# Window attention with v held in PE: probabilities divided before they are weighed, the norm's scale applied at the residual

## The reference, cut to what matters

```python
s = einsum('bnqgrd,bnkgd->bngrqk', q, k) * (HEAD_DIM ** -0.5)
s = where(mask, s, NEG_INF)
m = maximum(max(s, axis=-1, keepdims=True), sink)
p = exp(s - m)
w = p / (sum(p, axis=-1, keepdims=True) + exp(sink - m))
attn = einsum('bngrqk,bnkgd->bnqgrd', w, v)
...
mix = concatenate([rmsnorm(attn, norm_attn_out), rmsnorm(ssm, norm_ssm_out)], axis=-1)
x = x + mix @ w_out
```

## Time and profile before

| | |
|---|---|
| median of 3 runs | 3607.56 us (3603.56 to 3611.9) |
| the profiled execution | 3614.2 us, span of its trace 3612.4 us |
| mean granted clock of TensorE in it | 0.797 |
| weighing of step 0 to weighing of step 7 | 73.97 to 380.10 us |
| end of the last mixing of `mix_tokens` | 400.18 us |

### The profile page before, as it was taken

One profiled execution on the slowest core, in us unless ns is written; L12 is line 12 of the kernel. 1 busy time (PEld: TensorE's weight loads), 2 busy tenths in 40 slices (PEclk: granted clock), 3 DMA queues, 4 the chain that ended last, 5 costly groups with the idle time before them and its releaser, 6 DMA issues.

```text
span 3612.4 us, 35899 instructions
## 1 busy us (share of the span) xinstructions
PE 2437.9 (67%) x9537; PEld 1030.4 (29%) x9537; DVE 2217.7 (61%) x4968; ACT 1007.9 (28%) x3376; POOL 1335.4 (37%) x1236
## 2 busy tenths in 40 slices
PE   7999656268566755765676667566856775686676
PEld 4565344114112311321141114111411331142121
DVE  5322251756865785578567756875686579558754
ACT  1111021133233223322332333233223222332232
POOL 1000030034434444444444444444444444444532
PEclk8888677679778868986896689677967886897699
DMA  4111124099999999999999999999999999999998
GB/s 155 44 44 38 39 50 192 31 414 416 407 382 417 415 376 393 415 420 369 403 415 409 382 396 421 394 368 411 417 398 373 414 413 383 412 421 417 390 421 349
DMA packets 192622, 1212.41 MB, mean 336 GB/s; under 512 B 28952, under 2 KB 35416, under 8 KB 51688
## 3 DMA queue, kind: packets, MB, share of 16 engines
q0 software_dynamic: 156672, 1140.92, 77.9%
q1 hardware_dynamic: 35416, 69.28, 5.5%
q10 hardware_dynamic: 320, 0.07, 0.0%
HBM read 1194.51 MB, written 15.55 MB: 335 GB/s over the span
## 4 chain that ended last, share of the span: by engine, by line
DMA 30%; PE 22%; DVE 15%; issue 11%; ACT 4%; POOL 2%; SPq 0%; DVEq 0%; POOLq 0%; ACTq 0%; PEldq 0%
DMA uv_ring<-in_uv_table,idx 29%; PE ACC L1787 13%; PE TQ L1742 7%; DVE uv_ring L1630 5%; DVE S L1594 2%; DVE picks L1595 2%; DVE S L1593 2%; POOL uv_ring L1369 2%; PE OP L1723 1%; ACT dg L1463 1%; ACT dot L1456 1%; DMA wq<-in_w_query 1%; ACT dot L1446 1%; PE ACC L1777 0%; DVE pos L1525 0%
## 5 line engine op out<-in xcount | busy, mean ns | idle before, releaser
L1787 PE MATMUL ACC<-uv_ring,dg 128*64 128x512 f32 x4352 | 1485.8, 795 | 935.0 <-ACT dg L1463 934.0
L1369 POOL DMA_INDIRECT uv_ring<-in_uv_table,idx x1088 | 1264.9, 1163 | 1822.2 <-PE ACC L1787 1319.2
L1630 DVE CUSTOM_DVE_ANT_0 uv_ring<-uv_ring,xn 128x1024 f32<-128x1024 f32 x1088 | 1325.2, 1226 | 826.8 <-DMA uv_ring<-in_uv_table,idx 764.3
L1787 PEld LDWEIGHTS ACC<-uv_ring,dg 128*64 128x64 f32 x4352 | 345.0, 168 | 1955.9 <-ACT dg L1463 1422.0
L1446 ACT ACTIVATE dot<-dot 128x2 f32<-128x2 f32 x544 | 110.6, 203 | 1767.6 <-DVE dot L1630 1767.2
L1463 ACT ACTIVATE dg<-stack,dot 128x64 f32<-128x64 f32 x1088 | 328.5, 341 | 53.3
L1742 PEld LDWEIGHTS TQ<-glu_and_queries,wq 128*128 128x128 f32 x2304 | 267.8, 195 | 66.2 <-issue 66.2
L1742 PE MATMUL TQ<-glu_and_queries,wq 128*128 128x128 f32 x2304 | 281.9, 281 | 1.4 <-issue 1.2
L1456 ACT ACTIVATE dot<-gate,dot 128x1 f32<-128x1 f32 x1088 | 261.2, 287 | 17.7
L503 PE MATMUL PJ<-w_in,xT 128*128 128x512 f32 (+1 forms) x432 | 160.5, 532 | 1.6 <-DMA w_in<-in_w_in 1.6
L503 PEld LDWEIGHTS PJ<-w_in,xT 128*128 128x128 f32 x432 | 83.5, 194 | 80.6 <-issue 75.4
(11 more groups left out here) (318 smaller groups left out, 1760.3 us busy)
## 6 DMA issues: line engine op xcount, KB each, us to landing
uv_ring<-in_uv_table,idx POOLq DMA_INDIRECT x1088, 11.0
glu_and_queries<-in_w_glu SPq DMA_DIRECT2D x9, 1024.0 KB, 17.0
wq<-in_w_query SPq DMA_DIRECT2D x1, 8192.0 KB, 31.6
xt<-in_x SPq DMA_DIRECT2D x9, 512.0 KB, 3.5
xr<-scratch_x SPq DMA_DIRECT2D x9, 512.0 KB
w_in<-in_w_in SPq DMA_DIRECT2D x2, 2048.0 KB, 10.7
xk<-in_x SPq DMA_DIRECT2D x8, 512.0 KB, 3.3
scratch_x<-xk SPq DMA_DIRECT2D x8, 512.0 KB, 2.6
```

Source lines behind the costliest of these rows:

```text
L1369: pool.indirect_dma_start(out=ring[:, s_ % RING, :], out_offset=None, in_=a["uv_table"], in_offset=bass.IndirectOffsetOnAxis(ap=idx[:, s_: ...
L1630: V.tensor_tensor_reduce(row, row, xn[:, g, :], 1.0, 0.0, ALU.mult, ALU.add, dot[:, s_:s_ + 1]).then_inc(dots, 1)
L1787: ins = nc.tensor.matmul(ACC[GT * g:GT * (g + 1), b, :], dg[:, n % DG, :], ring[:, n % RING, D + 512 * b:D + 512 * b + 512], start=False, ...
```

## The change

Five things change together. (1) The weighing of v: PE holds v (a window's 128 keys by 64 of one group) and the turned probabilities stream, 512 columns at a time (four heads by 128 queries). There are 4 products in place of 16, and their result in `X` is already turned: 64 partitions for each group, (r, query) along the free side. So `turn_out` and its copy go. (2) The probabilities are divided before PE turns them: `normalise_probs` scales the 8 heads' 128x256 rows on DVE by `rden`, and PE's turning waits for `normed` where it waited for `probs_done`. (3) The norm's scale is applied where the residual is added (`scalar_tensor_tensor` with `rsa`). Its mean square comes from ACT's squares of `X` (`square_attention`) and four products of PE with a column of ones (`sum_squares`), between the scores and the mixing. (4) The scores are taken in the order group 0, group 1, group 0, and so on. (5) `g_attn` and the rows of `w_top` are laid out for the order (r, g), and `mix_samples` places its heads likewise, with as many transfers of the same sizes.

```diff
-        at2 = c.sb("at2", [P, AW])
-        aT = c.sb("aT", [P, AW // P, P])
+        sq = c.sb("sq", [P, REP, P])
+        aT = c.sb("aT", [P, REP, P])
+        ones = c.sb("ones", [P, 1])
         small = c.sb("small_a", [P, 8, HEADS])
         stat = c.sb("stat_a", [P, 8])
...
         weights, late = c.sem("weights_in"), c.sem("late_in")
...
                 load_tables(0, 0)
                 sp.dma_start(sink[:], a["sink"].to_broadcast([P, HEADS])).then_inc(late, 16)
...
                     rstd(t, ssx, msx, rsx, D, k["ssx_done"], k["msx_done"], k["rsx_done"])
 
                 def rstd_a(t):
-                    rstd(t, ssa, msa, rsa, AW, k["ssa_done"], k["msa_done"], k["rsa_done"])
...
 
                 def rotate(t, p):
 
@@ -306,15 +309,15 @@
                     k["roped"].mark(pool.tensor_tensor(x2, rt[:, 2], rt[:, 3], ALU.add))
 
                 def step(t, p, first=False, last=False):
+                    k["weighed"].held(pool, t - 1)
+                    k["v_kept"].mark(pool.tensor_copy(vb[:, p, :], pj[:, p, AW + KV * HD:U_COL]))
...
-                for n in ("ssx_done", "qkT_done", "probs_done", "ptr_act"):
+                for n in ("ssx_done", "qkT_done", "probs_done", "ptr_act", "sq_done"):
                     k[n].prime(act)
+
...
                     nc.scalar.activation(qT[:].rearrange("p r n -> p (r n)"), QK[:, 0:512], ACT.Copy)
                     k["qkT_done"].mark(nc.scalar.activation(kT[:, p, :], QK[:, 512:512 + P], ACT.Copy))
+                    if not first:
+                        square_attention(t - 1)
...
-                def divide(t):
+                def take_attention(t):
 
                     k["weighed"].of(dve, t)
-                    k["rden_done"].of(dve, t)
-                    k["at2_done"].of(dve, t - 1)
-                    k["at_done"].mark(nc.vector.tensor_tensor(
-                        at[:].rearrange("p (h d) -> p h d", d=HD), X[:].rearrange("p (h d) -> p h d", d=HD),
-                        bcast(rden, HD, 2), ALU.mult))
-                    k["at_done"].of(dve, t)
-                    k["a_turned"].of(dve, t - 1)
-                    k["ssa_done"].mark(nc.vector.tensor_tensor_reduce(at2[:], at[:], at[:], 1.0, 0.0,
-                                                                      ALU.mult, ALU.add, ssa))
-
-                def normalise_out(t):
-                    k["ssa_done"].of(dve, t)
-                    k["rsa_done"].of(dve, t)
-                    k["at2_done"].mark(nc.vector.tensor_scalar(at2[:], at[:], rsa, None, ALU.mult))
-
-                def take_out_columns(t):
-                    k["a_turned"].of(dve, t)
                     k["mixed"].of(dve, t - 1)
                     k["aT_done"].mark(nc.vector.tensor_tensor(
-                        aT[:], X[:].rearrange("p (k n) -> p k n", n=P), bcast(g_attn[:], P, 2), ALU.mult))
+                        aT[:], X[:].rearrange("p (r n) -> p r n", n=P), bcast(g_attn[:], P, 2), ALU.mult))
+
+                def mean_square(t):
+                    k["summed"].of(dve, t)
+                    k["rsa_done"].of(dve, t - 1)
+                    k["msa_done"].mark(nc.vector.tensor_scalar(msa, X[:, 0:1], 1.0 / AW, EPS, ALU.mult, ALU.add))
+
+                def normalise_probs(t):
+                    k["rden_done"].of(dve, t)
+                    for h in range(HEADS):
+                        ins = nc.vector.tensor_scalar(pr[:, h, :], pr[:, h, :], rden[:, h:h + 1], None, ALU.mult)
+                    k["normed"].mark(ins)
 
                 def add_residual(t, p):
                     k["mixed"].of(dve, t)
+                    k["rsa_done"].of(dve, t)
                     xk_in.of(dve, t)
                     for b in range(2):
                         half_row = xk[:, p, 512 * b:512 * b + 512]
-                        ins = nc.vector.tensor_tensor(half_row, PJ[:, b, :], half_row, ALU.add)
+                        ins = nc.vector.scalar_tensor_tensor(half_row, PJ[:, b, :], rsa, half_row, ALU.mult, ALU.add)
                     k["x1_done"].mark(ins)
 
                 def step(t, p, first=False, last=False):
                     if not first:
-                        divide(t - 1)
+                        take_attention(t - 1)
                     normalise(t + 1, 1 - p)
-                    if not first:
-                        normalise_out(t - 1)
                     take_columns(t + 1)
-                    if not first:
-                        take_out_columns(t - 1)
 
...
                     k["maxed"].mark(ins)
+                    if not first:
+                        mean_square(t - 1)
                     k["maxed"].of(dve, t)
                     nc.vector.tensor_scalar(nm, mx, -1.0, None, ALU.mult)
                     k["shifted"].mark(nc.vector.tensor_tensor(sd, sink[:], mx, ALU.subtract))
                     if not first:
                         add_residual(t - 1, 1 - p)
                     k["probs_done"].of(dve, t)
-                    k["at_done"].of(dve, t - 1)
+                    k["normed"].of(dve, t - 1)
                     k["den_done"].mark(nc.vector.tensor_tensor(den, rs, es, ALU.add))
                     k["den_done"].of(dve, t)
                     k["rden_done"].mark(nc.vector.reciprocal(rden, den))
+                    normalise_probs(t)
                     if first:
                         par.output_matrices(nc, dve)
...
-                take_out_columns(PT - 1)
+                take_attention(PT - 1)
+                mean_square(PT - 1)
                 add_residual(PT - 1, 1)
...
-                def turn_out(t):
-                    k["at2_done"].of(pe, t)
-                    for j in range(AW // P):
-                        ins = nc.tensor.transpose(X[:, j * P:(j + 1) * P], at2[:, j * P:(j + 1) * P], ident[:])
-                    k["a_turned"].mark(ins)
+                def sum_squares(t):
+                    k["sq_done"].of(pe, t)
+                    k["aT_done"].of(pe, t)
+                    for r in range(REP):
+                        ins = nc.tensor.matmul(X[:, 0:1], sq[:, r, :], ones[:], start=(r == 0), stop=(r == REP - 1))
+                    k["summed"].mark(ins)
...
                     turn_x(t + 1)
-                    if not first:
-                        turn_out(t - 1)
                     k["qkT_done"].of(pe, t)
-                    for h in range(HEADS):
+                    for h in (g * REP + r for r in range(REP) for g in range(KV)):
                         g, r = divmod(h, REP)
                         ins = nc.tensor.matmul(SC[:, h // 2, h % 2, :], qT[g * HD:(g + 1) * HD, r, :],
                                                kT[g * HD:(g + 1) * HD, :, :].rearrange("p a n -> p (a n)"),
                                                start=True, stop=True)
                     k["scored"].mark(ins)
                     if not first:
+                        sum_squares(t - 1)
                         k["xT_done"].of(pe, t + 1)
                         mix(t - 1)
                     project(t + 1)
-                    k["probs_done"].of(pe, t)
+                    k["normed"].of(pe, t)
...
-                    k["aT_done"].of(pe, t - 1)
-                    for h in range(HEADS):
-                        g = h // REP
-                        for w in range(2):
-                            ins = nc.tensor.matmul(X[:, h * HD:(h + 1) * HD], ptr[:, 2 * h + w, :],
-                                                   vb[:, w, g * HD:(g + 1) * HD], start=(w == 0), stop=(w == 1))
+                    k["msa_done"].of(pe, t - 1)
+                    for w in range(2):
+                        for g in range(KV):
+                            ins = nc.tensor.matmul(X[g * HD:(g + 1) * HD, :], vb[:, w, g * HD:(g + 1) * HD], ptr_g[:, g, w],
+                                                   start=(w == 0), stop=(w == 1))
                     k["weighed"].mark(ins)
...
-        "g_attn": np.ascontiguousarray(f["norm_attn_out"].reshape(AW // P, P).T),
+        "g_attn": np.ascontiguousarray(f["norm_attn_out"].reshape(AW)[cols[:AW]].reshape(AW // P, P).T),
+        "w_top": f["w_out"][0][cols[:AW]],
```

More of the change, by code:

```diff
@@ L163, in mix_tokens @@
         mx, nm, sd, es, rs, den, rden = (small[:, i, :] for i in range(7))
-        ssx, msx, rsx, ssa, msa, rsa = (stat[:, i:i + 1] for i in range(6))
+        ssx, msx, rsx, msa, rsa = (stat[:, i:i + 1] for i in range(5))
         PJ = c.ps("PJ", [P, 3, 512])
@@ L252, in _ @@
                 sp.dma_start(g_attn[:], a["g_attn"]).then_inc(late, 16)
-                sp.dma_start(w_top[:], a["w_out"][0:AW, :].rearrange("(k p) n -> p k n", p=P)).then_inc(late, 16)
+                sp.dma_start(w_top[:], a["w_top"].rearrange("(k p) n -> p k n", p=P)).then_inc(late, 16)
                 load_residual(0, 0)
@@ L273, in _ @@
             def _(pool):
-                for n in ("roped", "rsx_done", "msx_done", "v_kept", "rsa_done", "msa_done", "rope_mul"):
```

(21 more changed lines are left out.)

19 lines of the change are left out of this document (8 added, 11 removed).

## The result

The changed kernel takes 3523.59 us (median of 4 runs, 3523.02 to 3526.42), the kernel before took 3605.56 beside it (4 runs, 3598.88 to 3611.9): ratio 0.9774 (95% interval 0.9755 to 0.9794), 82.0 us less. The reason that I gave for the clock didn't hold.

What follows compares the result with a forecast made beforehand. PE was taken to bound the stage: with full clock, steps of 35.6 us for a mean 43.73 end it at 338.3 for 400.18, 61.9 us less; that gave 3545.7 us, stated as 3547, range 3539 to 3580.

Steps and rivals of the forecast that it cites:

- The reason that I gave for the clock: Steady fronts, weighing to mixing: full clock holds because the weighing streams 512 columns per instruction, with wide scores 3 us behind.
- Rival B: Clock still falls in each front, weighing to mixing: 6.1 us each, total 3589 (3558 to 3589 if partly); chance 0.27.
- C: Rival: array halves don't run together in weighing and scores; 2.5 us a step, 20 in all, 3567; chance 0.06.
- D: Rival: chained sums of squares between scores and mixing eat the gain at 1.1 us per instruction; 3613 at 1.2; chance 0.03.
- E: Rival: no change, since PE waiting for DVE absorbs the gain; 3607; chance 0.02.
- PE's wait in step 0: PE waits 5.86 us for DVE's matrices in step 0; claimed to stay near 6, at +0.4 us.
- back part: From mixing to the next weighing (mixing, projection, turning of the probabilities, copy wait): left alone by the change, 27.5 us.
- for new waits and for changes of the array's split: Allowance of 0.4 us in each steady full-clock step, included in the step of 35.6.
- the last step's 0.4: Last step: DVE idles 2.11 us before the projection, so 2.4 us of scalings are just not covered, +0.4.
- The end: Stage's last weighing, taking and squaring, sum and mixing: 13.0 us in the middle for the present 20.08, ending at 338.3.
- The parts put at nothing: DVE's eight scalings in a steady step, 2.4 to 2.8 us, claimed covered by DVE's 15.50 us idle before the projection.
- what PE gains moves all of them forward: Phases behind the stage start when it ends, so PE's gain there, 61.9 us, moves them all forward.

Runs made afterwards that it cites:

- experiment 3: Empty instructions at the start of POOL's program: three in the changed kernel, 3532.9 us (ratio 0.9794); 125 in the kernel before, 3591.33 us (0.9955).
- experiment 4: The changed kernel with its weighing cut into 64 products of 64 columns in place of 8 of 512: 3522.99 us, ratio 0.9762.
- experiment 6: The changed kernel with the old weighing's products (probabilities held, v streaming 64 columns), attention results not the reference's: 3563.7 us, ratio 0.9861.
- (5): The changed kernel with four more DVE passes over `X`, results unused, ahead of `take_attention`: 3555.27 us, ratio 0.9852.
- experiment 2: Score order alone: alternate groups put into the kernel before, 3588.05 us (ratio 0.9937); the old order put back into the changed kernel, 3535.45 us (0.9789).

## Why the prediction was right and where it was wrong

**Bound and course of the stage.** Right. PE is what the others wait for, the stage shortens by what PE gains, and the clock stays at 1.00 through all steady fronts, as the forecast had it. Rival B, the fall in each front, did not come; nor C, since the halves pair; nor D, since the sums of squares take 0.92, near the 0.95 of the weighing's load row and far from 1.1 us for each instruction; nor E. One sign missed: PE's wait in step 0 was to be near 6 us and was 9.64, since what PE does ahead got shorter by more than DVE's chain.

**The terms** at full clock, predicted and measured: weighing 1.87 and 1.87; wait for `xs` 1.74 and 1.51; turning 1.16 and 1.03; scores 2.0 and 1.92; sums 0.95 and 0.92; back part 27.5 and 27.47. Together 35.2 and 34.72; in addition I had put 0.4 "for new waits and for changes of the array's split", and nothing of that came. Six steps at 0.82 each (35.6 less their mean of 34.78) are 4.9 us, step 1 0.3, the last step's 0.4, and 1.2 from "the weighing of step 0 starts at 74.4", which was at 73.17 (that start lies anywhere from 71.9 to 76.3 in the traces of the changed kernel and of the variants that leave step 0 as it is). The end is 13.08 for 13.0. The last mixing ended at 331.48 for 338.3: **the stage gave 68.7 for the 61.9 of the sum**, 6.8 us of sizes, of which the six allowances of 0.4 for waits that no row showed are about a third. Three slips of the working don't change this: the middle of the end's own terms is 12.6 and not 13.0, the low end comes to some 3542 by its own terms and not 3540, and the 1.2 us for each instruction in rival D give some 3615 and not 3613. The parts put at nothing were hidden as said: the back part, in which DVE's eight scalings stand, takes 27.47 for 27.50, and the timelines of ACT

```profile
251.97 0.27 ACT L353 ACTIVATE kT<-SC 128x128 f32<-128x128 f32 x1
252.12 0.60 ACT L338 ACTIVATE sq<-X 128x512 f32<-128x512 f32 x1
```

and of DVE

```profile
250.78 0.69 DVE L412 TENSOR_TENSOR aT<-X,g_attn 128x512 f32<-128x512 f32 x1 [2.08 <-PE X L561]
251.38 0.74 DVE L388 TENSOR_SCALAR xs<-xt,stat_a 128x1024 f32<-128x1024 f32 x1
```

show the square done at 252.7, 2.4 us before the sums at 255.13 want it, and one pass of DVE ahead of `normalise` for two in the earlier trace rows.

**The step that failed** is in the first paragraph: "what PE gains moves all of them forward". The sum took the phases behind the stage as of fixed length. They took 22.6 less in the two traces, and some 13 less by the medians (82.0 less the stage's 68.7). The place of POOL's loop is shown to be worth 13 us of it in the traces of after, and 9 by the medians, and 15 by the medians of before: the change takes three instructions out of POOL's list ahead of it, experiment 3 puts them back or shifts before to the same pattern, and the retrieval follows both times. No row of before spoke of that as a term of the change, but the row of 9.99 us of idle POOL at each turn was there to be seen. Without this effect the kernel stands at 3532.9, still 6 below the range's low end: the 3545.7 of the sum less the stage's 6.8 is 3538.9, already at that end, and the rest is not explained. The low end was too near: it had a step of 35.2, and 34.78 came.

**The reason for the clock** was wrong though its outcome was right, and that part of the forecast was luck. I put it on the 512 columns of each instruction; experiment 4 has 64 and keeps the clock. And I read the fall at 299.60 as the usual one, while in five cases of seven it came during the weighing (experiment 6). What the runs bear out: before, the front was a weighing of 112 ns for each instruction, whose length goes with the 128 columns that are loaded and not with those that stream (115 ns with one column, 112 with 64), a wait of 2.35 us and turnings, and the clock fell; take back the weighing alone (experiment 6) or lengthen the wait alone (5), and it falls again. So of the 82 us some 40 hang on the weighing's form (3563.7 for 3523.59; the last mixing ends 38.9 later in its trace), of which 12 or so are its own length (1.7 for each step) and the rest is the clock.

**Two rules of the Trainium skill** ("TensorE: Matmul & The Clock Gate") bear on this. Its Part 4 (PE-mode transpose) says that the full clock doesn't engage for turnings. Here it stands at 1.00 for 245.7 us in which every step has 29 of them (5, 8 and 16), and the eight of x take 1.09 us for 1.97: the trace disagrees where dense work surrounds them. By the strict program order of Part 3 in the Trainium skill the alternation would have been worth eight slots in sixteen, by an estimate 8 x 0.22 = 1.8 us a step; experiment 2 measured 0.97, as twelve slots against eight give.

**Left open.** The 5.4 us between the stage and the retrieval: from the last mixing to the first product of ACC it is 333 us in before and both of its variants without empty instructions, 331 in before with 125 of them, and 327.5 to 330.3 in after and all variants of it, the one with three empty instructions among them (329.7); no run says what sets it. Why POOL's loop costs more at 202 than at 199 I didn't try. The change also moves the starts of the other engines' loops in the retrieval (PE's by 44 instructions, DVE's by 12, ACT's by 9); the empty instructions move POOL's alone, so that it counts is shown, and what the others' places are worth is not known. Nor do I know why the clock came back sooner in the kernel with alternate scores, for which the denser scores are an argument and not a proof.

## What to carry to other kernels

Look at what PE does in a stretch at low clock before pricing a change to it: in this kernel products that hold 128 columns to stream 64 cost their own length and, in all fronts but one, the clock of what follows, and so did a pause of some 3 us behind dense ones; each alone was enough to lose it. Look at several falls of the clock and not at one. When code ahead of a long loop changes its number of instructions, compare the idle time at that loop's turns on every engine before believing that a difference in the loop comes from the change. An allowance for waits that no row shows belongs in the range and not in the sum.

## What the runs showed of the hardware that I had not expected

- POOL was idle for 9.3 to 10.1 us at each of six turns of a loop that begins at its instruction 202 (8.6 to 10.2 in the changed kernel with three empty instructions), and for 3.6 to 4.5 and 3.0 to 3.9 us in two parts at 199 and at 327; over the retrieval that is 13 us between the traces of after, more than 0.3% of the kernel, for three empty instructions.
- Products that hold 64 columns on alternate halves of the array run in pairs down to 64 columns of stream: 64 of them in 2.01 us, 31 ns each. The same multiplications with 128 columns held took 32 instructions of 112 ns.
- Four one-column sums of squares that all add to one column of PSUM take 0.92 us for eight instructions, 115 ns each, beside 112 ns for an instruction of the old weighing with as many columns to load: the chain on one column costs nothing that shows.
- A pause 2.4 us longer (3.14 for 0.75) cost 4.5 us a step, since the clock went with it.
- The granted clock fell in the middle of a weighing in which PE was never idle: 2.30 us of it at 1.00, busy for 2.29, then 0.50.
